# Turning the router's slots after 28 expert units instead of 30, and one wait of VectorE ahead of its loop

## The reference

```python
q = (h @ wq).reshape(B, S, PEER_HEADS, 2, half)
s1 = einsum(q[..., 0, :], keys[:, 0]); s2 = einsum(q[..., 1, :], keys[:, 1])
v1, i1 = lax.top_k(s1, 16); v2, i2 = lax.top_k(s2, 16)
sc, j = lax.top_k(v1[..., :, None] + v2[..., None, :], 16)   # over 256 candidates
experts = i1[j // 16] * 128 + i2[j % 16]
gates = jax.nn.softmax(sc, axis=-1)                          # 8 heads x 16 slots
act = gelu(einsum('td,ted->te', ht, u[et]))
out = einsum('te,ted->td', gates * act, v[et])
```

## Time and profile before

| what | value |
|---|---|
| median of 3 runs | 2499.53 us |
| the profiled execution | 2501.45 us |
| its span | 2499.7 us |
| PE busy | 2391.0 us (96%) |
| DVE busy | 1651.4 us (66%) |
| ACT busy | 1161.2 us (46%) |
| POOL busy | 1006.4 us (40%) |
| mean granted clock of TensorE | 0.971 |

### The profile page before, as it was taken

The page is one execution under the profiler, slowest core; times in us unless marked ns, Lnnn a source line. Parts: engine busy times, 40 slices in busy tenths (PEclk is TensorE's granted clock), DMA queues, the critical chain, the costliest instruction groups (busy, mean ns, idle before and its releaser), DMA issues.

```text
span 2499.7 us, 51433 instructions
## 1 busy us (share of the span) xinstructions
PE 2391.0 (96%) x18346; PEld 2178.7 (87%) x18346; DVE 1651.4 (66%) x3049; ACT 1161.2 (46%) x1603; POOL 1006.4 (40%) x950
## 2 busy tenths in 40 slices
PE   7789999999999999999999999999999999899989
PEld 6779999999988888796899999998888888888987
DVE  5651899777788855532229987778886552335985
ACT  5434444434444455555344443434444554665444
POOL 4516798543333100022378884343330003654430
PEclk9889999999999999996899999999999999999999
DMA  4314555455555566552256655555556664444554
GB/s 141 106 35 143 160 180 182 148 155 165 157 167 167 167 193 193 168 160 60 61 160 181 179 164 157 165 155 167 166 166 180 193 193 136 134 120 138 169 156 151
DMA packets 106100, 383.58 MB, mean 153 GB/s; under 512 B 12432, under 2 KB 12704, under 8 KB 105632
## 3 DMA queue, kind: packets, MB, share of 16 engines
q1 hardware_dynamic: 104400, 379.13, 50.4%
q10 hardware_dynamic: 1616, 3.33, 0.4%
HBM read 381.37 MB, written 1.05 MB: 153 GB/s over the span
## 4 chain that ended last, share of the span: by engine, by line
PE 67%; DVE 13%; POOL 8%; issue 7%; ACT 3%; DVEq 1%; ACTq 0%; POOLq 0%
PE bank L1572 10%; PE bank L1574 10%; PE bank L1573 10%; PE bank L1483 9%; PE bank L1484 8%; PE bank L1486 8%; POOL w_lo L363 8%; PE bank L1746 4%; DVE sco L1117 2%; DVE big L1395 2%; DVE big L1075 1%; DVE big L1072 1%; DVE big L1401 1%; DVE sco L1098 1%; DVE w_lo L861 1%
## 5 line engine op out<-in xcount | busy, mean ns | idle before, releaser
L465 ACT ACTIVATE w_hi<-ring 128x1024 fp32r<-128x1024 f32 x719 | 758.2, 1057 | 789.5 <-PE bank L1574 419.7
L363 POOL TENSOR_TENSOR w_lo<-ring,w_hi 128x1024 fp32r<-128x1024 f32 x281 | 704.6, 2522 | 936.2 <-ACT w_hi L465 935.1
L1483 PE MATMUL bank<-x_hi,w_hi 128*128 128x256 f32 x3328 | 958.0, 288 | 38.9 <-ACT x_hi L478 17.5
L1484 PE MATMUL bank<-x_hi,w_lo 128*128 128x256 f32 x3328 | 945.2, 284 | 0.0
L1486 PE MATMUL bank<-x_lo,w_hi 128*128 128x256 f32 x3256 | 924.5, 284 | 0.0
L861 DVE TENSOR_TENSOR w_lo<-ring,w_hi 128x1024 fp32r<-128x1024 f32 x438 | 539.3, 1232 | 256.6 <-ACT w_hi L465 251.4
L1483 PEld LDWEIGHTS bank<-x_hi,w_hi 128*128 128x128 f32 x3328 | 643.6, 193 | 53.1 <-issue 24.2
L1484 PEld LDWEIGHTS bank<-x_hi,w_lo 128*128 128x128 f32 x3328 | 644.1, 194 | 0.0
L1486 PEld LDWEIGHTS bank<-x_lo,w_hi 128*128 128x128 f32 x3256 | 628.4, 193 | 0.0
L1572 PE MATMUL bank<-w_hi,x_hi 128*128 128x512 f32 x1112 | 440.2, 396 | 5.9 <-DVE x_lo L868 5.9
L1574 PE MATMUL bank<-w_lo,x_hi 128*128 128x512 f32 x1112 | 434.2, 391 | 0.0
(11 more groups left out here) (253 smaller groups left out, 2081.1 us busy)
## 6 DMA issues: line engine op xcount, KB each, us to landing
ring<-u_dram SPq DMA_DIRECT2D x256, 512.0 KB, 3.7
ring<-v_dram SPq DMA_DIRECT2D x256, 512.0 KB, 4.2
ring<-up_dram SPq DMA_DIRECT2D x44, 512.0 KB, 3.6
ring<-wq_dram SPq DMA_DIRECT2D x32, 512.0 KB, 3.6
ring<-sb_in_dram SPq DMA_DIRECT2D x31, 512.0 KB, 3.7
ring<-od_in_dram SPq DMA_DIRECT2D x25, 512.0 KB, 3.7
ring<-down_dram SPq DMA_DIRECT2D x22, 512.0 KB, 3.6
ring<-ev_in_dram SPq DMA_DIRECT2D x21, 512.0 KB, 3.6
```

Of the source, the lines that this page charges most:

```text
L363: pool.tensor_tensor(w_lo[:, k % RING, :], ring[:, k % RING, :], w_hi[:, k % RING, :].bitcast(F32), ALU.subtract).then_inc(g["lo_pool"], 1)
L465: A(w_hi[:, k % RING, :], ring[:, k % RING, :], ACT.Copy).then_inc(g["w_hi_done"], 1)
L1483: mm(dst, hi[:, rows[c]], xh[:, c, :], start=(c == 0), stop=False)
L1484: mm(dst, lo[:, rows[c]], xh[:, c, :], start=False, stop=False)
```

## The change

On TensorE the transposes move from behind unit 30 to behind unit 28, so four units stand between them and the first spread. On ScalarE the exponentials move from behind the eviction of unit 29 to behind that of unit 27. On VectorE the wait for 32 evicted units leaves the loop and stands ahead of it, thus ahead of the first two `low`.

```diff
-                unit_loop(29, lambda i, q: big[:, bass.ds(i * 1536 + q * 512, 512)], ACT.Gelu)
+                unit_loop(27, lambda i, q: big[:, bass.ds(i * 1536 + q * 512, 512)], ACT.Gelu)
                 for tb in range(TB):
                     act.wait_ge(g["gate_shifted"], TB * layer + tb + 1)
                     v = slot3[:, (2 * TB + tb) * P:(2 * TB + tb + 1) * P]
                     A(v, v, ACT.Exp).then_inc(g["gate_exped"], 1)
-                unit_loop(35, lambda i, q: big[:, bass.ds(i * 1536 + (29 * 512 + q * 512), 512)], ACT.Gelu)
+                unit_loop(37, lambda i, q: big[:, bass.ds(i * 1536 + (27 * 512 + q * 512), 512)], ACT.Gelu)
...
                 build(0)
                 build(1)
+                dve.wait_ge(g["units_out"], u[0] - 32)
                 with dve.Fori(0, groups // 3) as i:
                     for q in range(3):
                         low(k0 + 2 * q, i)
                         low(k0 + 2 * q + 1, i)
-                        if q == 0:
-                            dve.wait_ge(g["units_out"], u[0] - 32)
                         gate(q, i)
                         build(q + 2, i)
...
-                unit_loop(30)
+                unit_loop(28)
                 pe.wait_ge(g["slots_ready"], TB * (layer + 1))
...
                 last.then_inc(g["slots_turned"], 1)
-                unit_loop(2)
+                unit_loop(4)
```

## The result

The changed kernel takes 2514.43 us (median of 4 runs, 2510.2 to 2515.44) against 2500.06 us before (also 4 runs): 14.4 us or 0.54% slower, ratio 1.0054 with a 95% interval of 1.0041 to 1.0067. Run again beside other kernels, its ratio was 1.0044 (1.0028 to 1.0060). The mean of all 21 runs of it is 2513.0 us, that of the 89 runs of the kernel before which ran beside the experiments 2501.9 us: 11.1 us. (These 89 are without the four runs above, mean 2499.4 us, and the 11 of the first experiment, mean 2500.3; with them it would be 11.3 us.) The prediction had 2507.1 us, range 2502.5 to 2511.5, so +7.6 us. The sign and most of the cost in the routers (the stretch of each PEER layer in which the gates are made and turned) were right; half of the 14.4 us, and a third of the 11.1, were missing.

What follows compares the result with a forecast made beforehand. TensorE was taken to bound most of the kernel, so changes act only where it waits. The move's +5.5 us and the hoisted wait's +2.1 us gave +7.6 us on 2499.53, so 2507.1 us, range 2502.5 to 2511.5.

Steps and rivals of the forecast that it cites:

- What bounds the routers: Around the transposes, TensorE waits 1.29 us for VectorE's gates, then 2.84 us through ScalarE's stop at the exponential (first layer).
- Part 1: Both routers: two units less cover cost 11.52 us a layer, earlier gates return 8.73 and 8.81; net +5.50 us.
- Part 2: Ahead of VectorE's loop: the hoisted wait delays unit 33 by 1.2 and 0.9 us, together +2.1 us.
- Part 3: Behind the transposes: the clock falls and recovers after a similar stretch, no difference; bounds -4.2 to +4.2 us.
- The sum: Both routers: +5.5 us for the move and +2.1 us for the wait give +7.6 us.
- E: At the restart: the longer stop costs more clock, up to +4.2 us, 2511.3 us; chance 0.10.
- The base: Whole kernel: the median of the runs shown, 2499.53 us, to which +7.6 us was added.
- A: Behind the transposes: the clock stays up or recovers at once, -4.2 us against the sum, 2502.9 us; chance 0.12.
- B: VectorE's L1117: GpSimd did not slow it, so gates come as late as now, +25 us, 2524.7 us; chance 0.04.
- C: VectorE's loop: the wait inside cost more than its idle time shows, 3.6 us come back, 2503.5 us; chance 0.05.
- D: At the first spread: unit 33's `low` still hides, so the hoisted wait is free, 2505.0 us; chance 0.09.

Runs made afterwards that it cites:

- the first experiment: The kernel before run again with no edit; ratio 0.9992 (0.9983 to 1.0001), mean 2500.3 us.
- the move alone: Kernel before with transposes after 28 units and exponentials after 27, the wait still inside the loop; ratio 1.0022, mean +5.5 us.
- two shifts: Kernel before with 16 or 29 idle matmuls behind the first router's stream; ratios 1.0003 and 1.0008, means +1.1 and +2.2 us.
- the long program: Kernel before with three of the first 30 units written out instead of looped, order unchanged; ratio 1.0015, mean 2506.8 us, +4.9 us.
- the square above: Four kernels: before, only the wait hoisted (+5.5 us), only the units moved (+5.5 us), and both, the changed kernel (+11.1 us).
- the version with 31 units: Kernel before with transposes after 31 units, ScalarE's next piece ahead of the exponentials, unit 33's low parts ahead of the hoisted wait; 2494.79 us, ratio 0.9966.
- the high part first: Kernel before with ScalarE preparing w_hi of unit 31's first piece ahead of the exponentials; ratio 1.0000 (0.9989 to 1.0011).

## Why the prediction was wrong in size, point by point

- **What bounds the routers.** Right: the gates end the wait ahead of the transposes, ScalarE's stop at the exponential the one behind them, with the same 5.25 us.
- **Part 1, the move: +5.5 us.** Right in mechanism and near in size. From the eviction of unit 27 to the transposes it was 18.44 us (439.59 - 421.15) and is 9.69 (428.68 - 418.99); in the second layer 18.47 and 9.69. The gates are 8.75 and 8.78 us earlier, 8.73 and 8.81 were predicted. In the second layer the way was another: not the first L1117 but the L1111 ahead of it was held up by GpSimd's last subtraction (4.43 us; before it took 2.29 there and the eight L1117 13.70), and all eight L1117 took 2.78 us together; the sum came out the same. By the Trainium skill (SBUF — State Buffer, section "SBUF: two separate sides") the two engines exclude each other for whole instructions. This trace agrees, and so do two experiments: one subtraction more cost 2.20 us, and two units less took 4.47 us off the group before.
- **Part 2, the wait: +2.1 us.** The term measures 1.34 + 1.11 = 2.45 us (2.38 us behind the spread's start, from 1.04 and 1.27), and 1.25 + 0.96 = 2.21 between two kernels at equal low clock. Right: VectorE's wait and the `w_lo` behind it set unit 33, as said.
- **Part 3, the clock at the restart: no difference.** Right in sum: four units take 25.23 and 25.37 us, 2.19 and 2.33 over 23.04, beside 2.65 and 1.57 before. The clock fell earlier, in the longer stop, and cost the transposes 0.7 us, which ScalarE's restart hid.
- **The sum.** From the eviction of unit 27 to unit 33 the profiles show 41.01 against 37.36 and 41.15 against 36.55 us: +3.65 and +4.60, together 8.25 where the sum had 7.6.
- **The step that failed** is that the sum ended at the routers. Part 3 priced the clock only behind the stops that I was changing, and every other stage went in at nothing, rival E included, without a reason. Elsewhere the first profile has +6.7 us (14.9 - 8.25), the mean of 21 runs +2.7, and this is the price of 7.4 us more of low clock in the mixers (2.3 us by the slope of 0.31). A term of its own was due: the slices of the page before show a lowered clock in several of these stages, and the kernel before itself ranges over 11 us (2496.1 to 2507.1).
- **The base.** The sum was put on the median of the three runs shown, 2499.53 us, which lies 2.4 us below the mean of the 89 later runs, and the four runs of the result lie 1.4 us above the mean of all 21. So of the 7.3 us between 2507.1 and 2514.43 the cost itself has 3.5 (0.7 in the routers, 2.7 elsewhere), and 3.8 are the luck of seven runs. Put on 2501.9 us, the forecast would have been 2509.5 us and the upper end of the range 2513.9: the mean of 21 inside it, the median of four still outside.
- **The rivals.** A (the clock recovers at once) and B (the gates come as late as now, +25 us) fall by the rows above. C (the wait inside the loop has a price) falls: s0 and s1 are the same with and without it. D (the `low` still hides) falls by 1.51 us of wait for it in each layer, and 1.60 with the wait alone. E (the longer stop costs more clock) is the nearest in time, 2511.3 us, but falls as a cause: behind the restarts the units take 4.52 us more than their steady pace in both layers together, where they took 4.22 more before.

What stays open is why the mixers run longer at low clock in some kernels. The length of TensorE's program alone is not enough (the move alone has it, and -0.7 us), nor is a shift in time by itself (two shifts cost only themselves), and a change in the routers is not needed (the long program has them unchanged). In the square above it goes with the hoisted wait. The same kernel shows different values in ev, oq, sb_in, sb_ab and up_down from one profile to the next, which no experiment here controls.

## What to carry to other kernels

Moving a synchronization ahead in a stream uncovers work of a unit's length for each unit moved (5.76 us here). Before pricing it, ask which engine falls silent in the gap and whose work it had slowed: here VectorE's multiplications took 0.34 instead of 2.5 us each, and the loss was only the difference. A wait that is hoisted out of a loop delays all that stood ahead of it in the body, so move what others need first ahead of the wait, as the version with 31 units does. Where a kernel has several stages with a lowered clock, bound what they may do as a term of its own: here it was +2.7 us. And take the base from enough runs: with a spread of 11 us, the median of three was 2.4 us off.

## What the runs showed of the hardware that I had not expected

- A stage of 177.4 us takes 178.4 to 179.0 us with 3.4 us of low clock in it and 179.6 us with 6.8 (od; all fourteen profiles fit this), 0.3 to 0.5 us for each us; its instructions are the same. Over the whole kernel it is 0.31 us for each us of low clock (89 runs of one program).
- Writing out three units of a loop, with no change of order, made the kernel 0.15% slower (1.0006 to 1.0024), all of it outside the place that was written out.
- The transposes ran at 1.2 GHz after waits of 4.07 us (1.54 instead of 0.87 us), and so they did after 8.92 and 5.94 us with 26 units ahead of them. After waits of 1.29 and 0.84 us they had not, nor after 3.48 us in the second layer with the high part first (0.88 us); in its first layer, after 3.50 us, they took 0.98.
